# Conditioning products of a small hybrid decoder step: weights held, nine columns streamed, and inputs laid out before the launch

## The chip, the cores and the metric

The kernel runs on one core of a Trainium2 chip. The metric is device time of one execution in microseconds (us), as the median over several runs. The engines are named as the profile names them: PE (TensorE matmul), PEld (its weight loads), DVE (VectorE), ACT (ScalarE), POOL (GpSimd), SP (SyncE, which here only issues DMAs). All data are 32-bit floats.

## The reference

One step of a two-layer decoder on 288 tokens: 256 of a prompt and 32 of eight sequences with four steps each. Layer 0 mixes tokens with a short gated convolution, layer 1 with the RWKV-7 recurrence; behind each stands a product-key expert mixer (PEER). Every sub-layer is scaled, shifted and gated by a vector that depends on the sequence alone:

```
cs = silu(c)                                   # 9 conditioning vectors: 1 prompt, 8 sequences
m = cs @ w_ada[i] + b_ada[i]                   # (9, 1024) @ (1024, 6144), for each of 2 layers
sh_m, sc_m, gt_m, sh_f, sc_f, gt_f = split(m, 6)
h = rmsnorm(x, g_mix[i]) * (1 + sc_m) + sh_m
x = x + gt_m * mixer(h)                        # layer 0: conv, layer 1: RWKV-7
h = rmsnorm(x, g_ffn[i]) * (1 + sc_f) + sh_f
x = x + gt_f * peer_ffn(h)                     # 8 heads x 16 experts a token, rows of 1024 gathered
```

At the end stands one more norm. Outputs are x, the last inputs of the convolution, the last row of layer 1, and the RWKV states (16 heads of 64 x 64, for the prompt and for each sequence).

## The kernel before

Everything is kept with the model dimension on the 128 partitions, in DC = 8 chunks: X and H are [128, 8, 288]. So inputs that arrive as rows of tokens are turned by PE (a product with the identity) and copied out of PSUM, and outputs are turned back.

PE's work is a fixed list of groups (STAGES, line 72). Each group takes the next of four PSUM banks; `done` counts it ready, and ACT or DVE copies it out and frees the bank. Every engine walks the list in the same order. SP loads weight tiles of 1024 x 512 (2 MB) into W, a ring of four (WRING); a tile is loaded when the group that used the slot last is done (line 440).

The conditioning product is split over 24 weight tiles, twelve a layer, in stages ad0 to ad7 (ADA_PARTS, line 62). `ada` on PE (line 501) holds the nine conditioning vectors as weights and streams 512 columns of w_ada, eight chunks deep: L519, eight products a tile, and the trace counts two passes for each 32-bit product. The result has the nine vectors on partitions; ACT copies it to ADR (L967), PE turns it with four small products (L510, `turn`), and ACT adds the bias (L981).

The order is: `crow`, `x`, `par` (turning of inputs, L486 to L498), ad0 (6 tiles), norm 0 (`norm`, L532: eight products with ones), ad1 (8 tiles), the convolution's input projection `cin` (24 groups, `project`, L555), the expert keys turned (`turn_keys`, L540), ad2 (1 tile), output projection `cout`, the convolution's state rows turned (`cst`, L576, copied by ACT at L1040 and sent), norm 1, ad3 (1), the experts of layer 0, norm 2, ad4 (2), the RWKV projections rp, `sst` (last rows turned, L682), kp, vp, the low-rank stages lm and l2 (L691, L700), ad5 (1), kn (L706), ad6 (1), bn (L711), ad7 (4), and the recurrence: two prompt tiles of 128 tokens (stages tm, nm, sq; the final state is turned in `pso`, L860) and the sample tile. There `sq2` works through eight pairs of heads c in an order written out by hand (SQ2, line 87): state blocks arrive in RAW, are turned (L876) and copied by ACT to SS; `right`, `sa`, `y` (L884, L894/L867) and the state update `new0`, `new1` (L901) follow, DVE adds (L1783), and the new states are turned back (L907), copied by ACT to OUTB and sent. Then wo, turn_keys(1), norm 3, the experts of layer 1, norm 4, and `fin`: the result turned (L930), copied (L1243) and sent from ACT (L1247).

The experts gather rows of 4 KB through POOL's queue (L1859); DVE multiplies them (L1451) and PE sums them (L647).

Of the kernel before, what the change touches and what calls it, by code (L numbers as in the profile page):

```python
# [12 lines left out]
P = 128  # L13
# [44 lines left out]
PAR_ROWS = (P, ROWS["b_ada0"] + 48 - P, 48)  # L58
CR_COND, CR_CONV, CR_SHIFT, CR_N = 0, NCOND, NCOND + 2 * NSEQ, NCOND + 3 * NSEQ


ADA_PARTS = {"ad0": [(0, j) for j in range(6)], "ad1": [(0, j) for j in range(6, 10)] + [(1, j) for j in range(4)],
             "ad2": [(0, 10)], "ad3": [(0, 11)], "ad4": [(1, 4), (1, 5)], "ad5": [(1, 6)], "ad6": [(1, 7)],
             "ad7": [(1, j) for j in range(8, 12)]}


def ada_stage(name):
    return [(name, 2 * len(ADA_PARTS[name]))]
# [3 lines left out]
STAGES = [("crow", 1), ("x", DC), ("par", 1), ] + ada_stage("ad0") + [("nrm0", 1)] + ada_stage("ad1")  # L72
STAGES += [("cin", 24), ("kt0", 4)] + ada_stage("ad2") + [("cout", DC), ("cst", 2)]
STAGES += [("nrm1", 1)] + ada_stage("ad3") + [("hf0", 2), ("qa0", 4), ("se0", 1), ("qb0", 12), ("sc0", 9), ("ht0", 4), ("res0", DC)]
STAGES += [("nrm2", 1)] + ada_stage("ad4") + [("rp", DC), ("sst", 2), ("kp", DC), ("vp", DC), ("lm", 3), ("l2", 24)]
STAGES += ada_stage("ad5") + [("kn", DC)] + ada_stage("ad6") + [("bn", DC)] + ada_stage("ad7")
NM_STEPS, NM_STEPS_S = 21, 7
for _t in range(2):
    STAGES += [(f"tm{_t}", 6), (f"nm{_t}a", 2 * NM_STEPS)] + [("gn0", 2)] * (_t == 1)
    STAGES += [(f"nm{_t}b", 2 * NM_STEPS), (f"sq{_t}", 16)] + [("pso", 2)] * (_t == 1)  # L80
STAGES += [("tm2", 6), ("nm2a", 2 * NM_STEPS_S), ("gn1", 2), ("nm2b", 2 * NM_STEPS_S), ("sq2", 9 * DC), ("gn2", 2), ("wo", DC)]
STAGES += [("kt1", 4), ("nrm3", 1), ("hf1", 2), ("qa1", 4), ("se1", 1), ("qb1", 12), ("sc1", 9), ("ht1", 4), ("res1", DC)]
STAGES += [("nrm4", 1), ("fin", 6)]
# [4 lines left out]
for _c in range(-1, DC + 1):  # L88
    SQ2 += [("turn0", _c + 1), ("turn1", _c + 1), ("sa", _c), ("out0", _c - 1), ("out1", _c - 1),
            ("right", _c + 1), ("y", _c), ("new0", _c), ("new1", _c)]  # L90
# [30 lines left out]
def build(nc, a, out):  # L121
    with ExitStack() as ctx:
# [9 lines left out]
        PAR = sb("PAR", [3 * P])  # L132
# [27 lines left out]
        COUT = sb("COUT", [DC, 18])  # L160

# [32 lines left out]
        CROW2 = carve(4 * DC * TOK, [D])  # L194
        YT = carve(2 * DC * TOK, [3, D])
# [13 lines left out]
        ADR = (scr[:].rearrange("p a b -> p (a b)"), DG[:].rearrange("p a b -> p (a b)"))  # L209
# [51 lines left out]
        s_raw0, s_raw = sem("raw_zero"), [sem("raw_loaded0"), sem("raw_loaded1")]  # L261
# [13 lines left out]
        s_silu = sem("silu_ready")  # L275
        s_xready = sem("x_ready")
# [5 lines left out]
        s_crow = sem("conv_rows_ready")  # L282
        s_kt = sem("keys_turned")
# [21 lines left out]
        s_yt = sem("y_rows_ready")  # L305
# [5 lines left out]
        def weight_tiles(w, k, cols, group0, per):  # L311
            for j in range(cols // 512):
                tiles.append(([(None, w[:, j * 512:(j + 1) * 512].rearrange("(c p) m -> p c m", p=P))],
                              group0 + per * (j + 1) - 1))

        def ada_rows(j):

            return max(2 * j - 1, 0)

        def ada_cols(j, n):  # L320
            return 2 * j + 2 if j < n - 1 else 2 * n - 1
# [15 lines left out]
        WT["cin"] = len(tiles)  # L337
        weight_tiles(a["conv_w_in"][0], D, 3 * D, GROUP["cin"], 4)
        ada_tiles("ad2")
        WT["cout"] = len(tiles)  # L340
        weight_tiles(a["conv_w_out"][0], D, D, GROUP["cout"], 4)
        ada_tiles("ad3")
        WT["q0"] = len(tiles)
        weight_tiles(a["peer_wq"][0], D, 2 * D, GROUP["qa0"], 4)
        later_queries(0)
        ada_tiles("ad4")
        for name in ("wr", "wk", "wv"):
            WT[name] = len(tiles)
# [7 lines left out]
        tiles.append(([(lambda _: L2[0:LW_, 0, :], a["rwkv_w2"][0]), (lambda _: L2[0:LA_, 1, :], a["rwkv_a2"][0]),
                       (lambda _: L2[:, 2, :], a["rwkv_g2"][0])], GROUP["l2"] + 23))
        assert WT["wr"] % WRING == 2 and WT["l1"] % WRING == 0 and WT["l2"] % WRING == 1
        for name in ("ad5", "ad6", "ad7"):
            ada_tiles(name)  # L360
        WT["wo"] = len(tiles)
        weight_tiles(a["rwkv_wo"][0], D, D, GROUP["wo"], 4)
        WT["q1"] = len(tiles)
        weight_tiles(a["peer_wq"][1], D, 2 * D, GROUP["qa1"], 4)
# [46 lines left out]
        def _(sp):  # L411
            def rows_in(name, src, n):
                at = ROWS[name]
                sp.dma_start(PR[at % P:at % P + n, at // P, :], src).then_inc(s_par, 16)

# [5 lines left out]
            rows_in("g_mix", a["g_mix"].rearrange("l (c p) -> (l c) p", p=P), 16)  # L421
            rows_in("g_ffn", a["g_ffn"].rearrange("l (c p) -> (l c) p", p=P), 16)
            rows_in("g_final", a["g_final"].rearrange("(c p) -> c p", p=P), 8)
            rows_in("conv_k", a["conv_k"].rearrange("l w (c p) -> (l w c) p", p=P), 24)
            rows_in("rwkv_mix", a["rwkv_mix"].rearrange("l w (c p) -> (l w c) p", p=P), 48)
            for name in ("rwkv_w0", "rwkv_a0", "rwkv_k_k", "rwkv_k_a", "rwkv_lnw", "rwkv_lnb"):
                rows_in(name, a[name].rearrange("l (c p) -> (l c) p", p=P), 8)
            rows_in("rwkv_r_k", a["rwkv_r_k"].rearrange("l (c h) n -> (l c) (h n)", h=2), 8)
            rows_in("b_ada0", a["b_ada"][0].rearrange("(c p) -> c p", p=P), 48)
            rows_in("b_ada1", a["b_ada"][1].rearrange("(c p) -> c p", p=P), 48)  # L430
            def raw(c):

                for hp in range(2):
                    sp.dma_start(RAW[HS * hp:HS * (hp + 1), c % 2, :, HS * hp:HS * (hp + 1)],
                                 a["state_wkv"][0, :, 2 * c + hp].rearrange("b i j -> i b j")).then_inc(s_raw[c % 2], 16)

            for t, (parts, _) in enumerate(tiles):
# [3 lines left out]
                if t == WT["wo"]:  # L441

                    sp.wait_ge(s_raw0, 1)
                    for c in range(2):
                        raw(c)
# [5 lines left out]
                if t == WT["q1"]:  # L451
                    for c in range(2, DC):

                        sp.wait_ge(bank_ready, GROUP["sq2"] + SQ2.index(("turn1", c - 2)) + 1)
                        raw(c)
# [4 lines left out]
            sp.wait_ge(s_out, 16 * 3)  # L460
# [3 lines left out]
        def _(pe):  # L464
# [1470 lines left out]
```

## Time and profile before

| what | value |
|---|---|
| median of 3 runs | 2646.41 us (2644.27 to 2663.16) |
| the profiled execution | 2678.61 us |
| its span, first to last instruction | 2676.9 us |
| mean granted TensorE clock | 0.921 |
| PE busy | 2186.8 us (82%) |
| DVE busy | 1438.0 us (54%) |
| POOL busy | 1197.3 us (45%) |
| ACT busy | 567.2 us (21%) |
| DMA moved | 717 MB, of which the gathers 604 MB |

A busy PE says little by itself: its instructions overlap and their ends are modelled, so the time of a stretch is read from when the next stretch starts. The granted clock is a share of 2.4 GHz: 1.00 is 2.4 GHz, 0.50 is 1.2 GHz, and a figure between them is a stretch with some of each. The chain of waits is followed back from the last instruction, and gives at each step what the next one waited for.

### The profile page before, as it was taken

To read this page: it belongs to the slowest core of one execution; us is meant where nothing else is said; L and a number is where in the kernel's file an instruction comes from. 1 tells how busy PE (TensorE), PEld (TensorE's weight loads), DVE (VectorE), ACT (ScalarE), POOL (GpSimd) and SP (SyncE) were. 2 spreads that over 40 slices of the span, in tenths; PEclk is the share of its full clock that TensorE was granted. 3 is DMA by queue.
4 is the path that set the end of the run, shared out by engine and by line. 5 is a ranking of instruction groups with operands and counts; after the bars stand their busy time and mean duration, and the time that the engine had idled before them with its cause. 6 is when DMAs were issued, how large, how long until landed. Compare 5 with 4: busy or idle time off the path is not lost.

```text
span 2676.9 us, 28048 instructions
## 1 busy us (share of the span) xinstructions
PE 2186.8 (82%) x7875; PEld 1207.3 (45%) x7875; DVE 1438.0 (54%) x3397; ACT 567.2 (21%) x1250; POOL 1197.3 (45%) x1215
## 2 busy tenths in 40 slices
PE   7999976777778777899789998879676767787787
PEld 2276642323323322376279897657332223233234
DVE  0103466677777774322862443745666666777743
ACT  1200222222222221213222211221222222222212
POOL 2000247777777777300000000003577777777772
PEclk9999988989889898999889888989889898898999
DMA  9733569999999999543200000444799999999995
GB/s 320 270 139 133 209 238 386 376 405 410 410 410 410 410 409 405 222 142 131 74 9 1 1 1 5 111 150 147 263 378 378 372 375 388 410 410 410 409 399 195
DMA packets 242643, 717.22 MB, mean 268 GB/s; under 512 B 39673, under 2 KB 45057, under 8 KB 242557
## 3 DMA queue, kind: packets, MB, share of 16 engines
q0 software_dynamic: 165888, 604.05, 58.2%
q1 hardware_dynamic: 62212, 105.00, 11.5%
q10 hardware_dynamic: 14456, 7.06, 1.0%
q8 instruction: 49, 0.80, 0.1%
q14 instruction: 38, 0.30, 0.0%
HBM read 712.38 MB, written 3.65 MB: 267 GB/s over the span
## 4 chain that ended last, share of the span: by engine, by line
PE 59%; DMA 23%; issue 7%; DVE 7%; POOL 2%; ACT 2%; ACTq 0%; DVEq 0%; POOLq 0%; SPq 0%
PE ps L647 24%; PE ps L555 14%; DMA ARENA<-in_peer_v,CURV 11%; DMA ARENA<-in_peer_u,CURU 10%; PE ps L519 6%; PE ps L775 5%; POOL ARENA L1859 2%; PE ps L757 1%; ACT DG L1110 1%; PE ps L617 1%; DVE ARENA L1598 1%; DVE W L1710 1%; PE ps L851 1%; PE ps L825 1%; PE ps L532 1%
## 5 line engine op out<-in xcount | busy, mean ns | idle before, releaser
L647 PE MATMUL ps<-ARENA,DG 128*128 128x512 f32 x2304 | 1140.4, 644 | 386.6 <-ACT DG L1110 259.1
L1859 POOL DMA_INDIRECT ARENA<-in_peer_u,CURU x576 | 584.7, 1015 | 1209.2 <-DVE GX L1421 1017.8
L1451 DVE SCALAR_TENSOR_TENSOR ARENA<-ARENA 128x1024 f32<-128x1024 f32 x576 | 703.5, 1225 | 434.7 <-DMA ARENA<-in_peer_u,CURU 433.2
L647 PEld LDWEIGHTS ps<-ARENA,DG 128*128 128x128 f32 x2304 | 447.8, 204 | 1078.1 <-issue 662.5
L1859 POOL DMA_INDIRECT ARENA<-in_peer_v,CURV x576 | 596.8, 1036 | 228.4 <-issue 139.4
L1110 ACT ACTIVATE DG<-ident,CF 128x128 f32<-128x128 f32 x576 | 219.8, 399 | 825.1 <-PE ps L647 718.9
L555 PE MATMUL ps<-H,W 128*128 128x288 f32 x1024 | 252.1, 409 | 2.8 <-DVEq L1789 2.8
L555 PEld LDWEIGHTS ps<-H,W 128*128 128x128 f32 x1024 | 195.8, 192 | 57.1 <-DVEq L1789 3.0
L519 PE MATMUL ps<-W,CT 128*9 128x512 f32 x384 | 170.4, 598 | 0.0
L775 PE MATMUL ps<-W 128*128 128x128 f32 (+1 forms) x1088 | 127.3, 281 | 0.0
L775 PEld LDWEIGHTS ps<-W 128*128 128x128 f32 (+1 forms) x1088 | 125.1, 196 | 2.3 <-issue 0.9
L555 PE MATMUL ps<-ARENA,W 128*128 128x288 f32 x512 | 124.9, 406 | 0.0
L555 PEld LDWEIGHTS ps<-ARENA,W 128*128 128x128 f32 x512 | 97.0, 190 | 26.6
L967 ACT ACTIVATE W<-ps 128x512 f32<-128x512 f32 (+2 forms) x97 | 55.9, 578 | 231.7 <-PE ps L775 170.7
L967 ACT ACTIVATE ARENA<-ps 128x512 f32<-128x512 f32 (+4 forms) x106 | 54.5, 543 | 197.7 <-PE ps L555 82.7
L1718 DVE TENSOR_TENSOR W<-W,ps 128x512 f32<-128x512 f32 (+1 forms) x76 | 50.6, 666 | 71.5 <-PE ps L775 71.0
L519 PEld LDWEIGHTS ps<-W,CT 128*9 128x9 f32 x384 | 33.5, 91 | 121.9 <-issue 121.6
L757 PE MATMUL ps<-ARENA 64*128 64x128 f32 (+1 forms) x480 | 60.5, 316 | 22.8 <-DVEq L1261 21.1
L1511 DVE TENSOR_TENSOR ARENA<-ARENA,ps 128x1024 f32 (+1 forms) x36 | 44.0, 1221 | 63.1 <-PE ps L647 58.3
L1064 ACT ACTIVATE GX<-GX 128x16 f32<-128x16 f32 x36 | 7.8, 216 | 327.5 <-DVE GX L1421 327.5
L757 PEld LDWEIGHTS ps<-ARENA 64*128 64x128 f32 (+1 forms) x480 | 53.6, 215 | 29.3 <-DVEq L1261 25.9
L1540 DVE SCALAR_TENSOR_TENSOR ARENA<-ARENA,PAR,H 128x288 f32<-128x288 f32 x48 | 21.8, 516 | 81.6 <-PE ps L555 80.6
(281 smaller groups left out, 1646.1 us busy)
## 6 DMA issues: line engine op xcount, KB each, us to landing
W<-in_w_ada SPq DMA_DIRECT2D x24, 2048.0 KB, 8.1
W<-in_peer_wq SPq DMA_DIRECT2D x8, 2048.0 KB, 8.2
W<-in_conv_w_in SPq DMA_DIRECT2D x6, 2048.0 KB, 7.9
ARENA<-in_peer_u,CURU POOLq DMA_INDIRECT x576, 6.6
ARENA<-in_peer_v,CURV POOLq DMA_INDIRECT x576, 6.6
W<-in_conv_w_out SPq DMA_DIRECT2D x2, 2048.0 KB, 7.8
W<-in_rwkv_wr SPq DMA_DIRECT2D x2, 2048.0 KB, 24.9
W<-in_rwkv_wk SPq DMA_DIRECT2D x2, 2048.0 KB, 8.6
```

What stands on the lines that cost most here:

```text
L519: m = pe.matmul(o[0:NCOND, :], CT[:, k, 0:NCOND], W[:, t % WRING, k, :], start=(k == 0), stop=(k == DC - 1))
L532: m = pe.matmul(o[:, 0:TOK], ones[:], SQ[:, c, :], start=(c == 0), stop=(c == DC - 1))
L555: m = pe.matmul(o[:, 0:TOK], W[:, t % WRING, k, (m0 % 4) * P:(m0 % 4 + 1) * P], rhs[:, k, :], start=(k == 0), stop=(k == DC - 1))
L647: m = pe.matmul(ps[:, 4 + 2 * e + i, :], DG[:, k % NDIAG, :], RVV[:, k % RING, i * 512:(i + 1) * 512], start=(k == 0), stop=(k == TOPK - 1))
L757: m = pe.matmul(o[0:n, j * n:(j + 1) * n], head(ops[0], h), head(ops[1], h), start=True, stop=True)
L775: m = pe.matmul(o[0:n, j * n:(j + 1) * n], l[:, j, :], r[:, j, :], start=True, stop=True)
L967: act.activation(dst, src(o), func, **kw).then_inc(free, 1)
L1110: act.activation(DG[:, k % NDIAG, :], ident[:], ACT.Copy, scale=CF[:, e, k:k + 1]).then_inc(s_diag, 1)
L1451: v.scalar_tensor_tensor(RU[:, k % RING, :], RU[:, k % RING, :], 1.0, h, ALU.mult, ALU.mult, accum_out=ZB[:, e, k:k + 1]).then_inc(s_z, 1)
L1511: v.tensor_tensor(oa, oa, ps[:, 4 + 2 * e:6 + 2 * e, :].rearrange("p b n -> p (b n)"), ALU.add).then_inc(acc_free, 1)
L1718: V.do(v.tensor_tensor(dst, dst, o, ALU.add))
L1859: pool.indirect_dma_start(ring[:, k % RING, :], None, tab, bass.IndirectOffsetOnAxis(ap=idx[:, k:k + 1], axis=0)).then_inc(landed[k % RING ...
```

## The change

The conditioning product is turned round: 128 x 128 blocks of w_ada are held as weights and the nine vectors are streamed, four blocks of outputs by eight chunks, that is 32 products of nine columns a tile. The result has the outputs on partitions, so `turn`, ADR and ACT's copy go. The 24 tiles are spread anew: 4 before norm 0, 2 behind it, then after each of the six tiles of `cin` 2, 2, 2, 1, 1, 1, then 1 (ad8), 2 (ad9), 1, 1 and 4 (ad10 to ad12).

kernel() lays out all inputs on the host: weight tiles with 16 KB in one piece for each partition, x, conditioning vectors, keys and parameters already turned, and the sequences' states as blocks of 128 x 1024 with zeros in place. So the stages crow, x, par, kt, cst, sst, pso, turn, out and fin go, with their copies; outputs leave as they lie on the partitions and are turned on the host. In `sq2` five groups are left for each c. SP issues the last output from H in four pieces, each as two chunks of H are ready.

```diff
-ADA_PARTS = {"ad0": [(0, j) for j in range(6)], "ad1": [(0, j) for j in range(6, 10)] + [(1, j) for j in range(4)],
-             "ad2": [(0, 10)], "ad3": [(0, 11)], "ad4": [(1, 4), (1, 5)], "ad5": [(1, 6)], "ad6": [(1, 7)],
-             "ad7": [(1, j) for j in range(8, 12)]}
+ADA_PARTS = {"ad0": [(0, j) for j in range(4)], "ad1": [(0, 4), (0, 5)], "ad2": [(0, 6), (0, 7)], "ad3": [(0, 8), (0, 9)],
+             "ad4": [(0, 10), (0, 11)], "ad5": [(1, 0)], "ad6": [(1, 1)], "ad7": [(1, 2)], "ad8": [(1, 3)],
+             "ad9": [(1, 4), (1, 5)], "ad10": [(1, 6)], "ad11": [(1, 7)], "ad12": [(1, j) for j in range(8, 12)]}
...
+STAGES = ada_stage("ad0") + [("nrm0", 1)] + ada_stage("ad1")
+for _j in range(CIN):
+    STAGES += [(f"cin{_j}", 4)] + ada_stage(f"ad{2 + _j}")
+STAGES += [("cout", DC), ("nrm1", 1)] + ada_stage("ad8")
...
-    SQ2 += [("turn0", _c + 1), ("turn1", _c + 1), ("sa", _c), ("out0", _c - 1), ("out1", _c - 1),
-            ("right", _c + 1), ("y", _c), ("new0", _c), ("new1", _c)]
+    SQ2 += [("sa", _c), ("right", _c + 1), ("y", _c), ("new0", _c), ("new1", _c)]
...
+            sp.dma_start(PAR[:], a["par"]).then_inc(s_par, 16)
+            def states(c):
+                sp.dma_start(SS[:, c % 2].rearrange("p s n -> p (s n)"), a["state_wkv"][c]).then_inc(s_raw[c % 2], 16)
...
-                        sp.wait_ge(bank_ready, GROUP["sq2"] + SQ2.index(("turn1", c - 2)) + 1)
-                        raw(c)
+                        sp.wait_ge(s_kept, c - 1)
+                        states(c)
...
+                if t == WT["q1"] + 1:
+                    for i in range(2):
+                        sp.wait_ge(s_stout[i], 16 * (DC // 2))
...
+            for c in range(0, DC, 2):
+                sp.wait_ge(s_hf, c + 2)
+                sp.dma_start(out["y"][:, c:c + 2, :], H[:, c:c + 2, :]).then_inc(s_out, 16)
...
-                    o = group(stage, ada_rows(j))
-                    for k in range(DC):
-                        m = pe.matmul(o[0:NCOND, :], CT[:, k, 0:NCOND], W[:, t % WRING, k, :], start=(k == 0), stop=(k == DC - 1))
+                    o = group(stage, j)
+                    for m4 in range(4):
+                        for k in range(DC):
+                            m = pe.matmul(o[:, m4 * NCOND:(m4 + 1) * NCOND], W[:, t % WRING, k, m4 * P:(m4 + 1) * P], CT[:, k, 0:NCOND],
+                                          start=(k == 0), stop=(k == DC - 1))
                     done(m)
-                    if j > 0:
-                        turn(j - 1)
-                turn(n - 1)
...
-            project("cin", "cin", 24, H, norm_of=0)
-            turn_keys(0)
-            ada("ad2")
+            for j in range(CIN):
+                project(f"cin{j}", f"cin{j}", 4, H, norm_of=0 if j == 0 else None)
+                ada(f"ad{2 + j}")
...
+            act.dma_start(CT[:], a["cond"]).then_inc(s_cr, 16)
+            act.dma_start(X[:], a["x"]).then_inc(s_x, 16)
...
+                                v.wait_ge(s_raw[c % 2], 16 * (c // 2 + 1))
+                                if c >= 2:
+                                    v.wait_ge(s_stout[c % 2], 16 * (c // 2))
...
+                        v.wait_ge(s_shr, 32)
```

## Rows read from the trace of the kernel before

**Rows 1.** Chain of waits, 0 to 230 us: start us, length us, what.
```profile
3.62 10.47 DMA ARENA<-in_x_sample
...
21.91 14.90 PE ps L519 x32
37.16 6.96 PE ps L519 x16
...
67.19 4.08 PE ps L532 x16
...
130.09 93.32 PE ps L555 x384
```

**Rows 2.** DMA issues of the first 1.25 us: size, us from issue to landing.
```profile
W<-in_w_ada SPq DMA_DIRECT2D x1, 2048.0 KB, 13.1
```

**Rows 3.** Chain of waits, 220 to 420 us.
```profile
233.27 31.24 PE ps L555 x128
264.51 0.45 PE ps L576 x4
...
267.51 4.13 PE ps L532 x16
...
281.46 1.02 PE ps L592 x8
```

**Rows 4.** Chain of waits, 1060 to 1400 us.
```profile
1133.01 13.85 PE ps L519 x32
...
1179.23 0.87 PE ps L682 x8
...
1312.68 14.64 PE ps L519 x32
...
1343.09 2.77 PE ps L733 x24
```

**Rows 5.** Chain of waits, 1441 to 1475 us: 128 x 128 weights, 64 columns streamed.
```profile
1443.33 3.57 PE ps L825 x32
```

**Rows 6.** L775, weight loads ns min/median/max: 1360 to 1365 us, then 1410 to 1415 us.
```profile
L775 PEld LDWEIGHTS ps<-W x20: 286/333/333, 1360.9 to 1364.9; 128*128 128x128 f32 x20
...
L775 PEld LDWEIGHTS ps<-W x46: 186/192/218, 1409.8 to 1415.0; 128*128 128x128 f32 x46
```

**Rows 7.** Windows: stretch, length, busy us (count) PE, PEld, DVE, ACT, POOL, clock, DMA, GB/s.
```profile
20.00:40.00 20.00, 20.00 (x50) 4.93 (x51) 1.48 (x5) 4.55 (x14) 0.35 (x3) 1.00 1.05 373
...
1295.00:1300.00 5.00, 1.91 (x8) 1.14 (x6) 5.00 (x1) 0.56 (x4) 0.00 (x0) 1.00 1.00 356
1300.00:1305.00 5.00, 0.00 (x0) 0.00 (x0) 5.00 (x1) 0.00 (x0) 0.00 (x0) 0.56 0.16 58
1305.00:1310.00 5.00, 1.52 (x3) 1.17 (x4) 4.49 (x6) 0.00 (x0) 0.00 (x0) 0.50 0.00 0
1310.00:1315.00 5.00, 5.00 (x10) 1.78 (x9) 3.68 (x6) 0.00 (x0) 0.00 (x0) 0.57 0.00 0
...
1360.00:1365.00 5.00, 5.00 (x24) 4.78 (x24) 1.47 (x3) 0.89 (x2) 0.00 (x0) 0.50 0.01 3
...
1443.00:1447.00 4.00, 4.00 (x37) 3.99 (x36) 0.00 (x0) 1.25 (x3) 0.00 (x0) 1.00 0.00 0
...
1668.00:1672.00 4.00, 3.73 (x64) 3.40 (x62) 2.73 (x10) 0.00 (x0) 0.00 (x0) 0.50 0.00 0
```

**Rows 8.** Sample tile: chain of waits, then the window 1702 to 1733.5 us.
```profile
1679.05 11.56 DMA ARENA<-in_state_wkv
...
1702.00:1733.50 31.50, 28.93 (x193) 19.42 (x193) 26.13 (x48) 9.26 (x17) 0.00 (x0) 1.00 0.27 59
```

**Rows 9.** Norm 3 in the chain of waits, then the end in the timeline.
```profile
1793.32 4.16 PE ps L532 x16
...
2666.08 3.52 DVE L1310 SCALAR_TENSOR_TENSOR H<-X,PAR,rstd 128x288 f32<-128x288 f32 x8
...
2674.52 0.34 ACTq L1247 DMA_DIRECT2D out<-ARENA  x1
```

More of the change, by code:

```diff
@@ L57 @@
 NROWS = _rows()
-PAR_ROWS = (P, ROWS["b_ada0"] + 48 - P, 48)
-CR_COND, CR_CONV, CR_SHIFT, CR_N = 0, NCOND, NCOND + 2 * NSEQ, NCOND + 3 * NSEQ
-ADA_PARTS = {"ad0": [(0, j) for j in range(6)], "ad1": [(0, j) for j in range(6, 10)] + [(1, j) for j in range(4)],
-             "ad2": [(0, 10)], "ad3": [(0, 11)], "ad4": [(1, 4), (1, 5)], "ad5": [(1, 6)], "ad6": [(1, 7)],
-             "ad7": [(1, j) for j in range(8, 12)]}
-def ada_stage(name):
[L68 to L76, printed above, removed]
+CR_CONV, CR_SHIFT, CR_N = NCOND, NCOND + 2 * NSEQ, NCOND + 3 * NSEQ
+QUAD = 32
+CIN = 6
+ADA_PARTS = {"ad0": [(0, j) for j in range(4)], "ad1": [(0, 4), (0, 5)], "ad2": [(0, 6), (0, 7)], "ad3": [(0, 8), (0, 9)],
+             "ad4": [(0, 10), (0, 11)], "ad5": [(1, 0)], "ad6": [(1, 1)], "ad7": [(1, 2)], "ad8": [(1, 3)],
+             "ad9": [(1, 4), (1, 5)], "ad10": [(1, 6)], "ad11": [(1, 7)], "ad12": [(1, j) for j in range(8, 12)]}
+def ada_stage(name):
+    return [(name, len(ADA_PARTS[name]))]
+STAGES = ada_stage("ad0") + [("nrm0", 1)] + ada_stage("ad1")
+for _j in range(CIN):
+    STAGES += [(f"cin{_j}", 4)] + ada_stage(f"ad{2 + _j}")
+STAGES += [("cout", DC), ("nrm1", 1)] + ada_stage("ad8")
+STAGES += [("hf0", 2), ("qa0", 4), ("se0", 1), ("qb0", 12), ("sc0", 9), ("ht0", 4), ("res0", DC)]
+STAGES += [("nrm2", 1)] + ada_stage("ad9") + [("rp", DC), ("kp", DC), ("vp", DC), ("lm", 3), ("l2", 24)]
+STAGES += ada_stage("ad10") + [("kn", DC)] + ada_stage("ad11") + [("bn", DC)] + ada_stage("ad12")
 NM_STEPS, NM_STEPS_S = 21, 7
@@ L304, in build, with weight_tiles @@
         s_acc = sem("expert_rows_ready")
-        s_yt = sem("y_rows_ready")
         dve_step, pool_step = sem("dve_step"), sem("pool_step")
         tiles = []
[L311 to L321, printed above, removed]
+        def weight_tiles(w, group0, per):
+            for j in range(w.shape[0]):
+                tiles.append(([(None, w[j].rearrange("p (c m) -> p c m", c=DC))], group0 + per * (j + 1) - 1))
         def later_queries(layer):
@@ L355, in build @@
         WT["l2"] = len(tiles)
[L356 to L359, printed above, removed]
+        tiles.append(([(lambda _: L2, a["lora_out"].rearrange("p (c m) -> p c m", c=3))], GROUP["l2"] + 23))
+        assert WT["q0"] % WRING == 0 and WT["wr"] % WRING == 2 and WT["l1"] % WRING == 0 and WT["l2"] % WRING == 1
@@ L360, in build @@
+        for name in ("ad10", "ad11", "ad12"):
             ada_tiles(name)
         WT["wo"] = len(tiles)
-        weight_tiles(a["rwkv_wo"][0], D, D, GROUP["wo"], 4)
+        weight_tiles(a["rwkv_wo"], GROUP["wo"], 4)
         WT["q1"] = len(tiles)
-        weight_tiles(a["peer_wq"][1], D, 2 * D, GROUP["qa1"], 4)
+        weight_tiles(a["peer_wq"][4:8], GROUP["qa1"], 4)
         later_queries(1)
@@ L700, in rwkv @@
                         done(pe.matmul(o[:, 0:TOK], L2[0:n, i, c * P:(c + 1) * P], LM[0:n, i, :], start=True, stop=True))
-                ada("ad5")
+                ada("ad10")
                 pe.wait_ge(s_kksq, 1)
@@ L706, in rwkv @@
                     done(pe.matmul(o[:, 0:TOK], BLK, XI1[:, c, :], start=True, stop=True))
-                ada("ad6")
+                ada("ad11")
                 pe.wait_ge(s_rk, 1)
@@ L853, in rwkv @@
                                 done(m)
-                        if tile == 1:
-                            evac(sq, 12)
-                            evac(sq, 13)
-                            for q in range(2):
-                                o = group("pso", q)
-                                for j in range(4):
-                                    m = pe.transpose(o[:, j * P:(j + 1) * P], SB[:, 4 * q + j, :], ident[:])
-                                done(m)
                     else:
@@ L902, in sample_step @@
                                               SAVM[0:2 * n, 4 * half:4 * half + 4, :].rearrange("p s n -> p (s n)"), start=True, stop=True)
-                            else:
-                                half = int(kind[-1])
-                                evac("sq2", SQ2.index((f"new{half}", c)))
-                                for j in range(4):
-                                    m = pe.transpose(o[:, j * P:(j + 1) * P], NEW[:, c % 2, 4 * half + j, :], ident[:])
                             done(m)
@@ L973, in ada @@
             def ada(stage, between={}):
-                n = len(ADA_PARTS[stage])
-                def columns(j):
-                    o, free = take(stage, ada_cols(j, n))
+                for j, (layer, part) in enumerate(ADA_PARTS[stage]):
+                    o, free = take(stage, j)
                     for m4 in range(4):
-                        layer, m0 = ADA_PARTS[stage][j][0], 4 * ADA_PARTS[stage][j][1]
-                        m = act.activation(ADA[:, layer, m0 + m4, :], o[:, m4 * NCOND:(m4 + 1) * NCOND], ACT.Identity,
-                                           bias=col(f"b_ada{layer}", m0 + m4))
+                        m = act.activation(ADA[:, layer, 4 * part + m4, :], o[:, m4 * NCOND:(m4 + 1) * NCOND], ACT.Identity,
+                                           bias=col(f"b_ada{layer}", 4 * part + m4))
                     m.then_inc(free, 1)
-                for j in range(n):
-                    copy(stage, ada_rows(j), ADR[j % 2][0:NCOND, :], lambda o: o[0:NCOND, :])
-                    if j > 0:
-                        columns(j - 1)
                     if j in between:
                         between[j]()
-                columns(n - 1)
-            taken("par", 0)
+            act.wait_ge(s_par, 16)
             def squares(i):
@@ L1003, in _ @@
             ada("ad0")
-            def keys(layer):
-                for i in range(4):
-                    o, free = take(f"kt{layer}", i)
-                    act.activation(KT[:, i // 2, 4 * (i % 2):4 * (i % 2) + 4, :],
-                                   o.rearrange("p (h k) -> p h k", h=4), ACT.Copy).then_inc(s_kt, 1)
-                    act.wait_ge(s_kt, 4 * layer + i + 1)
-                    act.sem_inc(free, 1)
             def root_and_h(i):
-                if i == 3:
-                    keys(1)
                 act.wait_ge(s_ms, i + 1)
@@ L1026, in _ @@
             ada("ad1")
-            for m in range(16):
-                o, free = take("cin", m)
-                dst = (BG if m < 8 else CG)[:, m % 8, :]
-                act.activation(dst, o[:, 0:TOK], ACT.Copy).then_inc(free, 1)
-                if m == 15:
-                    act.wait_ge(free, (GROUP["cin"] + m) // BANKS + 1)
-                    act.sem_inc(s_gates, 1)
-            keys(0)
-            ada("ad2")
-            for i in range(2):
-                o, free = take("cst", i)
-                if i == 0:
-                    act.wait_ge(s_cv, 1)
-                act.activation(CROW[0:18, i * 512:(i + 1) * 512], o[0:18, :], ACT.Copy).then_inc(free, 1)
-                act.wait_ge(free, (GROUP["cst"] + i) // BANKS + 1)
-            act.dma_start(out[2].rearrange("l b w d -> (l b w) d"), CROW[0:2, :]).then_inc(s_crow, 16)
-            act.dma_start(out[5].rearrange("l b w d -> (l b w) d"), CROW[2:18, :]).then_inc(s_crow, 16)
+            for j in range(CIN):
+                if j < 4:
+                    dst = BG if j < 2 else CG
+                    for m in range(4):
+                        o, free = take(f"cin{j}", m)
+                        act.activation(dst[:, 4 * (j % 2) + m, :], o[:, 0:TOK], ACT.Copy).then_inc(free, 1)
+                    if j == 3:
+                        for m in range(4):
+                            taken("cin3", m)
+                        act.sem_inc(s_gates, 1)
+                ada(f"ad{2 + j}")
+            act.wait_ge(s_cout, 1)
+            act.dma_start(out["conv"], COUT[:]).then_inc(s_crow, 16)
             def experts(layer):
@@ L1048, in experts @@
                 if layer == 0:
[L1049 removed]
+                    ada("ad8")
                 for i in range(2):
@@ L1124, in rwkv @@
                     if stage == "rp":
-                        for i in range(2):
-                            copy("sst", i, CROW2[0:NCOND, i * 512:(i + 1) * 512], lambda o: o[0:NCOND, :])
-                            taken("sst", i)
-                        act.dma_start(out[3][0], CROW2[0:1, :]).then_inc(s_shr, 16)
-                        act.dma_start(out[6][0], CROW2[1:NCOND, :]).then_inc(s_shr, 16)
+                        act.wait_ge(s_sh, 1)
+                        act.dma_start(out["shift"], SHIFT).then_inc(s_shr, 16)
                 copy("lm", 0, LM[0:LW_, 0, :], lambda o: o[0:LW_, 0:TOK], ACT.Tanh)
@@ L1144, in rwkv @@
                 act.activation(XI1, AF, ACT.Square).then_inc(s_kksq, 1)
-                ada("ad5")
+                ada("ad10")
                 act.wait_ge(s_kkn, 1)
                 act.activation(XI0, XI0, ACT.Sqrt).then_inc(s_kkr, 1)
-                ada("ad6")
+                ada("ad11")
                 def exps():
@@ new lines, in rwkv @@
+                            for j in (12, 13):
+                                taken("sq1", j)
+                            act.dma_start(out["wkv_prompt"], SB).then_inc(s_shr, 16)
+                    else:
+                        for c in range(DC):
+                            for k in ("new0", "new1"):
+                                taken("sq2", SQ2.index((k, c)))
+                            act.dma_start(out["wkv_sample"][c], NEW[:, c % 2].rearrange("p s n -> p (s n)")).then_inc(s_stout[c % 2], 16)
@@ L1233, in _ @@
             root_and_h(2)
-            ada("ad4")
+            ada("ad9")
             rwkv()
@@ L1238, in _ @@
             root_and_h(4)
-            for tile in range(3):
-                n = P if tile < 2 else NS_TOK
-                for i in range(2):
-                    o, free = take("fin", 2 * tile + i)
-                    act.activation(YT[0:n, tile, i * 512:(i + 1) * 512], o[0:n, :], ACT.Copy).then_inc(s_yt, 1)
-                    act.wait_ge(s_yt, 2 * tile + i + 1)
-                    act.sem_inc(free, 1)
-                dst = out[0][0, tile * P:(tile + 1) * P, :] if tile < 2 else out[1].rearrange("b t d -> (b t) d")
-                act.dma_start(dst, YT[0:n, tile, :]).then_inc(s_out, 16)
         @block.vector
@@ L1792, in _ @@
             experts(0)
+            gains("ad8", (2,))
             norm(2)
             rwkv()
-            v.wait_ge(s_stout[0], 16 * DC)
-            v.wait_ge(s_stout[1], 16 * DC)
+            for i in range(2):
+                v.wait_ge(s_stout[i], 16 * (DC // 2))
             experts(1)
```

303 lines of the change are left out of this document (94 added, 209 removed).

## The prediction

> **What bounds the kernel now.** I read the chain of waits first, stage by stage, since no engine is the limit throughout. From 22 to 265 us it is PE almost without a break: 14 conditioning tiles, the norm's sum, then `cin` with 93.3 us and, behind one more conditioning tile, `cout` with 31.2 us [rows 1, 3]. A conditioning tile is 16 passes in 6.96 us and a turn of 0.35 us (36.81 to 37.16), so 7.3 us [rows 1]. DMA is not what ends the waits there: at 373 GB/s a 2 MB tile takes 5.6 us [rows 7]. The two gather loops, most of the span, are left alone by the change. Between them lies layer 1 without its experts, where two conditioning tiles (13.85 us) and four (1312.68 to 1343.09, 30.4 us) stand in the chain [rows 4]. The other two, ad5 and ad6, lie beside DVE's work. So 21 of the 24 tiles are on the path, and what one costs decides. The clock view is then the one that matters: it gives PE 1.00 in the dense stretches and 0.50 in others [rows 7].
>
> **The new tile at full clock.** 32 products of two passes are 64 passes, each with a 128 x 128 weight load and nine columns. The nearest row with as many loads is L825, 64 columns: 32 passes in 3.57 us, 0.112 us each, and its loads are no faster where fewer columns stream, so the load is the limit [rows 5]. 64 x 0.112 = 7.15 us, as much as before: the turn goes, nothing else is won.
>
> **The new tile's clock.** Here I see the loss. Before, a pass streamed 512 columns; now it streams nine, for a load that is 14 times as wide, so PE's array sees 576 columns a tile instead of 8192. What such a stretch is granted no row shows. L825's stretch, 64 columns behind each load, keeps 1.00 (1443 to 1447). But from 1668 to 1672 us PE is busy 3.73 of 4.00 us with 64 narrow products (32 columns, 32 or 64 rows) and stays at 0.50 [rows 7]. Being busy is not what raises the clock; streaming much is the nearer reading, and a stream of nine columns is further down than anything that kept 1.00. I take 0.50.
>
> The price there: L775's passes come 24 in 5 us at 0.50, 0.21 us each [rows 7], and its loads take 286 to 333 ns instead of 186 to 192 [rows 6]. I take 0.213 a pass, 13.6 us a tile. Bounds: 0.112 if the load keeps its pace; 0.172 by the shortest loads' ratio (286/186 x 0.112); 0.24 for twice 0.112 and the nine columns behind it.
>
> The Trainium skill ("TensorE: Matmul & The Clock Gate", section LDWEIGHTS) gives a load's time by its columns alone, about columns/1.2 ns, without the clock. For 128 that is 107 ns, near the 112 measured at full clock; it would make a tile 6.8 us at either clock. The longer loads at 0.50 [rows 6] speak against it, though those passes also stream more.
>
> Changes of the clock cost too. PE ends at about 1296.9 us (1.91 busy of the stretch from 1295) and the clock falls at 1300.6 (0.56 over 1300 to 1305): I let 3.7 us, 33 passes, stay fast at the start of a block. PE starts again at 1308.5 (1.52 busy up to 1310), and 1.00 comes back at 1314.3 (0.57 over 1310 to 1315) [rows 7]; I take 5 us at half clock, 2.5 us lost, for each dense stage behind a conditioning block. A block of two tiles is then 3.7 + 95 x 0.213 = 23.9 us, one of one tile 3.7 + 31 x 0.213 = 10.3 us.
>
> **The head.** x, its turning and the rows' turning go, so PE waits for tile 0 alone. It lands 13.1 us after its issue at 0.8 us [rows 2], with the same neighbours in the queues (x, keys): start at 13.9 instead of 21.9 us. Then ad0 4 x 13.6 = 54.4; norm 0 4.1 + 2.3 = 6.4; ad1 23.9; six `cin` tiles 93.3 + 6 x 2.5 = 108.3; blocks 3 x 23.9 + 3 x 10.3 = 102.6. Sum 309.5 us against 233.3 [rows 3]: **+76.2**. The loads, 5.6 us a tile, and ACT's and DVE's work hide behind this. If PE were fast, they still would.
>
> **From cout to rp.** `cout` loses 2.5. `cst` goes: ACT's two copies and two issues held its squares back, so norm 1's sum ended 7.1 us after `cout` (264.5 to 271.6) [rows 3]; without them the last chunk's residual, square and two passes take 2.3: -4.8. ad8 lies beside the norm's work on DVE and ACT, which is all but 1.0 us (copy and turn) of the 9.8 from 271.6 to 281.5 [rows 3]; 2.3 us behind `cout` only its first 12 passes are fast, and 1.4 + 52 x 0.213 = 12.5 us is later than those 9.8 (+2.7). The queries start slow (+2.5): +5.2. ad9: 23.9 instead of 15.0 (1133.0 to 1148), and 2.5 for rp: +11.4. `sst`: -0.9 [rows 4].
>
> **ad10 to ad12.** ad10 and ad11, 10 to 14 us each, still fit beside DVE's work, for which PE waits there today (none of 1300 to 1305 [rows 7]). ad12 follows bn, which runs slow already: 54.4 instead of 30.4, and 2.5 behind it: +26.5. At full clock it would gain 30.4 - 28.6 = 1.8.
>
> **Recurrence, keys, tail.** `pso` and two issues on ACT: -2.5. In `sq2` a round (four in the window, 7.9 us each) loses the turns, but DVE is busy 26.1 of the 31.5 us, 6.5 a round [rows 8]; I take 7.2 with the gaps between its instructions. The stall of 11.6 us for a state behind two weight tiles stays in part, since SP sends the tiles first. Fewer columns a round may also lower the clock. From -9 to +4; I take -4. DVE's new waits (state in, state out, s_shr) have `gated` and `masked` queued behind them; the data are due a round or more earlier. Turning the keys held norm 3's sum back, so that all its 16 passes (4.16 us) stood behind the last square [rows 9] instead of the last two, and ACT's copy before them (0.5): -4.0. At the end H is complete at 2669.6 (DVE 3.52 us from 2666.08), then one issue and a landing of about 2.5 us, 2672.4 instead of 2676.9: -4.5 [rows 9].
>
> **Sum.** 76.2 + 2.5 - 4.8 + 5.2 + 11.4 - 0.9 + 26.5 - 2.5 - 4 - 4 - 4.5 = +101 us. The profiled execution took 2678.6 us; with it 2779.7. It lies 32 us above the median of the runs shown, so the forecast is **2747 us**. At 0.172 a pass the sum is +55 (2701), at 0.24 +132 (2778).
>
> **Rivals.** *The loads count as activity and PE stays at 1.00.* For it: L825's stretch, dense in loads, keeps 1.00 with 64 columns [rows 5, 7]; against: 1668 to 1672. Then the head is 13.9 + 28.6 + 2.5 + 4.1 + 14.3 + 93.3 + 64.4 = 221.1 (-12.2); with -4.8, ad8 -1.0, ad9 -0.7, sst -0.9, ad12 -1.8, pso -2.5, sq2 -8, keys -4, tail -4.5 it is -40: 2606 us, faster. The point from which it decides: whether 64 loads with nine columns behind each hold the clock.
>
> *The clock falls, but a load keeps 0.112 us.* Only the slow starts are lost: head +5.3, cout +2.5, ad8 +1.5, ad9 +1.8, ad12 +0.7, the rest as in the forecast: -9, 2637 us. The row on L775's loads is against it [rows 6]. The rule of the Trainium skill's page cited above would give this one.
>
> *Loads as short as in the turn.* L510 loads nine rows and streams nine columns; four take 0.35 us [rows 1]. If a pass took 0.09, tiles would be 5.6 us, no less than their DMA, and the whole some 30 us under the first rival. Turning and multiplying load differently in L825; little speaks for it.
>
> **Chances.** Forecast 0.62 (its own range 2695 to 2775), clock kept 0.19, load's pace kept 0.14, short loads or something else 0.05. The measurement of this kernel tells about 1% (26 us) from no change. Faster by more than that: 0.22 (the first and the last rival); within: 0.13; slower: 0.65. The range from 2625 to 2775 us leaves out the first and last rivals.
>
> **What would show it.** Right: the windows over ad0 and over the blocks in `cin` show 0.50 and 64 passes in some 13.6 us; `cin` groups start at 0.48 us a pass and go to 0.24; ad12 takes some 54 us; the experts' loops are unchanged. Wrong: 1.00 in ad0, or passes of 0.112 us at 0.50, or PE waiting for weight tiles, which would make the load and not PE the limit.

## The result, and the profile after

The changed kernel takes 2760.09 us (median of 4 runs, 2741.33 to 2776.47) against 2654.78 us for the kernel before measured beside it: a ratio of 1.0408, 95% interval 1.031 to 1.0506. The forecast was 2747 us. Slower, by about the size forecast. The profiled execution is the quickest of the four (span 2739.4 us, mean granted clock 0.876 instead of 0.921).

Chain of waits of the changed kernel (start us, length us, what). L459 is the conditioning product, L487 `project`, L472 the norm's sum; the rows answer to [rows 1, 3, 4, 9].

```profile
0.83 8.26 DMA CT<-in_cond
...
9.63 54.75 PE ps L459 x256
...
70.24 22.77 PE ps L459 x128
93.02 18.53 PE ps L487 x64
111.55 23.09 PE ps L459 x128
...
301.44 33.95 PE ps L487 x128
335.39 3.88 PE ps L472 x16
339.27 8.55 PE ps L459 x64
347.82 1.80 PE ps L518 x8
...
1190.61 23.50 PE ps L459 x128
...
1379.45 51.81 PE ps L459 x256
...
1876.23 3.89 PE ps L472 x16
```

Four tiles of ad0 take 54.75 us, 13.7 a tile. A block of two tiles inside `cin` takes 23.1 us where two tiles took 14.6 before [rows 1], and the dense tile behind a block takes 18.5 instead of 15.6 us (a sixth of the 93.32 us of [rows 1]); from 94 to 98 us, in the first of these, the clock is 0.50.

Windows of the same kernel (stretch, length, busy us with count for PE, PEld, DVE, ACT, POOL, then clock, DMA share, GB/s): ad0, the beginning of ad1 and its middle.

```profile
20.00:50.00 30.00, 30.00 (x143) 30.00 (x142) 0.00 (x0) 1.49 (x8) 0.26 (x3) 1.00 0.63 258
72.00:74.00 2.00, 2.00 (x20) 2.00 (x20) 1.93 (x3) 0.00 (x0) 0.00 (x0) 1.00 0.00 0
86.00:88.00 2.00, 2.00 (x11) 2.00 (x11) 0.00 (x0) 0.00 (x0) 0.00 (x0) 0.50 0.02 8
```

And the weight loads of line 459 (ns min/median/max), in ad0, at the beginning of ad1 and in its middle:

```profile
L459 PEld LDWEIGHTS ps<-CT,W x95: 333/333/334, 29.8 to 49.9; 128*128 128x128 f32 x95
L459 PEld LDWEIGHTS ps<-CT,W x37: 192/192/332, 70.9 to 74.9; 128*128 128x128 f32 x37
L459 PEld LDWEIGHTS ps<-CT,W x39: 333/333/333, 83.8 to 91.9; 128*128 128x128 f32 x39
```

ad1 shows the whole mechanism: right behind the dense norm, at 72 us, the clock is 1.00, a load takes 192 ns and the passes come 0.112 us apart (37 loads from 70.9 to 74.9 us); at 86 us, with PE busy all the while, the clock is 0.50, a load takes 333 ns and the passes come 0.213 us apart (39 loads from 83.8 to 91.9 us). The dense tile behind starts at half clock too. In ad0 the clock column prints 1.00, but loads (333 ns) and passes (54.75 us / 256 = 0.214 us) are those of 0.50. Experiments 1 and 2 below print 1.00 there too, one with fast passes and one with slow ones, so at the start of the span the column is no measurement; the load's length is.

A part of the difference isn't the change's. First and last start of the gather loops' products, before (line 647) and after (line 573):

```profile
L647 PE MATMUL ps<-ARENA,DG x1152: 592/592/1222, 378.5 to 1120.1; 128*128 128x512 f32 x192
L647 PE MATMUL ps<-ARENA,DG x1152: 592/592/1222, 1903.8 to 2650.5; 128*128 128x512 f32 x192
```

```profile
L573 PE MATMUL ps<-ARENA,DG x1152: 592/592/1222, 446.2 to 1178.0; 128*128 128x512 f32 x192
L573 PE MATMUL ps<-ARENA,DG x1152: 592/592/1222, 1987.9 to 2717.7; 128*128 128x512 f32 x192
```

The loops took 741.6 + 746.7 = 1488.3 us in the execution profiled before and 731.8 + 729.9 = 1461.7 after, with the same code. Over the ten profiles of this study they sum to between 1457 and 1512 us, with no relation to the conditioning. So I compare spans without the two loops: 2676.9 - 1488.3 = 1188.6 before, 2739.4 - 1461.7 = 1277.7 after, **+89 us**, where the forecast's sum was +101.

### The profile page after: what moved, and what is told of

Read it like the earlier page. It is cut to its first block, busy times and chain, and to the rows that moved or that the text cites. A ratio compares the mean times of both kernels' runs of the same rounds, so it can differ in the third digit from the quotient of the medians.

```text
span 2739.4 us, 29426 instructions
## 1 busy us (share of the span) xinstructions
PE 2285.5 (83%) x8688; PEld 1450.2 (53%) x8688; DVE 1432.4 (52%) x3385; ACT 526.4 (19%) x1173; POOL 1165.5 (43%) x1215
## 4 chain that ended last, share of the span: by engine, by line
PE 66%; DMA 19%; DVE 7%; issue 5%; POOL 1%; ACT 1%; DVEq 0%; POOLq 0%; ACTq 0%; SPq 0%
PE ps L573 28%; PE ps L487 14%; DMA ARENA<-in_peer_v,CURV 10%; PE ps L459 10%; DMA ARENA<-in_peer_u,CURU 9%; PE ps L693 5%; POOL ARENA L1672 1%; PE ps L675 1%; ACT DG L965 1%; PE ps L472 1%; PE ps L543 1%; PE ps L787 1%; DVE ARENA L1413 1%; DVE W L1523 1%; PE ps L769 1%
## 5 line engine op out<-in xcount | busy, mean ns | idle before, releaser
L1672 POOL DMA_INDIRECT ARENA<-in_peer_u,CURU x576 | 591.4, 1027 | 1307.2 <-DVE GX L1238 1112.0
L1672 POOL DMA_INDIRECT ARENA<-in_peer_v,CURV x576 | 558.4, 969 | 229.3 <-issue 145.3
L459 PE MATMUL ps<-CT,W 128*128 128x9 f32 x1536 | 288.2, 334 | 9.6 <-ACT CT L840 9.6
L459 PEld LDWEIGHTS ps<-CT,W 128*128 128x128 f32 x1536 | 289.3, 296 | 11.0 <-issue 9.6
L487 PE MATMUL ps<-H,W 128*128 128x288 f32 x1024 | 268.3, 427 | 2.8 <-DVEq L1601 2.8
L487 PEld LDWEIGHTS ps<-H,W 128*128 128x128 f32 x1024 | 205.3, 202 | 61.9 <-DVEq L1601 3.0
L487 PE MATMUL ps<-ARENA,W 128*128 128x288 f32 x512 | 129.6, 418 | 0.0
L487 PEld LDWEIGHTS ps<-ARENA,W 128*128 128x128 f32 x512 | 100.4, 197 | 28.4
L845 ACT ACTIVATE W<-ps 128x512 f32<-128x512 f32 (+2 forms) x81 | 46.5, 574 | 192.8 <-PE ps L693 172.0
L675 PE MATMUL ps<-ARENA 64*128 64x128 f32 (+1 forms) x480 | 59.4, 310 | 24.0 <-DVEq L1084 22.6
L845 ACT ACTIVATE ARENA<-ps 128x512 f32<-128x512 f32 (+3 forms) x86 | 43.7, 526 | 182.8 <-PE ps L487 85.2
L856 ACT ACTIVATE ADA<-ps,PAR 128x9 f32<-128x9 f32 x96 | 17.8, 269 | 268.1 <-PE ps L459 268.1
```

The costliest lines, as they stand in the source:

```text
L459: m = pe.matmul(o[:, m4 * NCOND:(m4 + 1) * NCOND], W[:, t % WRING, k, m4 * P:(m4 + 1) * P], CT[:, k, 0:NCOND], start=(k == 0), stop=(k == ...
L487: m = pe.matmul(o[:, 0:TOK], W[:, t % WRING, k, (m0 % 4) * P:(m0 % 4 + 1) * P], rhs[:, k, :], start=(k == 0), stop=(k == DC - 1))
L675: m = pe.matmul(o[0:n, j * n:(j + 1) * n], head(ops[0], h), head(ops[1], h), start=True, stop=True)
L845: act.activation(dst, src(o), func, **kw).then_inc(free, 1)
L1672: pool.indirect_dma_start(ring[:, k % RING, :], None, tab, bass.IndirectOffsetOnAxis(ap=idx[:, k:k + 1], axis=0)).then_inc(landed[k % RING ...
```

## The experiments

All are edits of the changed kernel. `cout` starts at 301.4 us there; that mark shows the head without the loops' scatter.

**1. Streaming more than is needed.** The nine vectors repeated 14 times as the moving operand; the copies are computed and not read.

```diff
+REP = 14
...
-m = pe.matmul(o[:, m4 * NCOND:(m4 + 1) * NCOND], W[:, t % WRING, k, m4 * P:(m4 + 1) * P], CT[:, k, 0:NCOND],
+m = pe.matmul(o[:, m4 * REP * NCOND:(m4 + 1) * REP * NCOND].rearrange("p (r n) -> p r n", r=REP),
+              W[:, t % WRING, k, m4 * P:(m4 + 1) * P], CT[:, k, 0:NCOND].unsqueeze(1).broadcast_to([P, REP, NCOND]),
               start=(k == 0), stop=(k == DC - 1))
...
```

> The changed kernel with the nine vectors streamed 14 times over behind each weight block (126 columns a pass instead of 9); nothing else differs. My theory: the narrow stream let the clock fall and the load takes 0.213 us a pass only because of the clock, so with 126 columns the granted clock is 1.00 in the conditioning blocks, a pass takes 0.112 us, a tile 7.2 us instead of 13.7, cout starts near 217 us instead of 301, ad12 takes 29 us instead of 52, and the whole is about 127 us below the changed kernel (some 2633 us), level with the kernel before or faster. Rival: 128-column loads back to back cost 0.213 us whatever streams behind them: cout at 301 us or later, no gain.

Measured: 2615.58 us (median of 4, 2609.30 to 2656.12), ratio to the kernel before 0.982 (95% interval 0.9728 to 0.9913; so for the ratios below). Chain of waits:

```profile
1.73 18.21 DMA W<-in_w_ada
19.99 21.70 PE ps L460 x192
41.69 3.88 PE ps L474 x16
45.57 14.29 PE ps L460 x128
59.86 15.53 PE ps L489 x64
...
217.30 31.04 PE ps L489 x128
...
1280.69 28.58 PE ps L460 x256
```

Windows of ad0, in its first 4 us and the next 4:

```profile
10.00:14.00 4.00, 4.00 (x21) 4.00 (x20) 0.00 (x0) 1.71 (x6) 3.20 (x13) 1.00 1.02 431
14.00:18.00 4.00, 4.00 (x38) 4.00 (x38) 0.00 (x0) 1.06 (x4) 3.13 (x14) 1.00 1.06 451
```

`cout` starts at 217.3 us, a tile takes 7.14, ad12 28.6. Fourteen times the stream made each pass half as long, 0.112 us, which is also what a pass of nine columns takes while the clock is up (ad1 of the changed kernel): in these runs the load alone sets the pass, and the stream decides at which clock the load runs. The rival (such loads cost 0.213 us whatever follows) falls. The dense tile behind a block is back at 15.5 us. Outside the loops the kernel is 37 us below the one before: what the forecast's first rival gave for a clock that stays up (-40).

**2. Half as many copies**: the same edit with 7 for 14.

> The same with seven copies, 63 columns a pass. My theory: like 126 columns, since the 64-column stretch of the recurrence kept 1.00: cout near 217 us, tile 7.2 us, some 2633 us. Rival: the clock falls gradually with the columns, so the blocks show a figure between 0.50 and 1.00 and cout starts between 230 and 290 us.

Measured: 2641.36 us, ratio 0.9963 (0.9922 to 1.0003). Chain of waits, then a window in ad0, one in ad1, and the loads of the same two stretches:

```profile
9.72 54.84 PE ps L460 x256
...
70.15 14.24 PE ps L460 x128
...
241.82 31.10 PE ps L489 x128
```

```profile
20.00:50.00 30.00, 30.00 (x142) 30.00 (x143) 0.00 (x0) 1.49 (x8) 0.25 (x3) 1.00 0.64 260
70.00:84.00 14.00, 14.00 (x128) 14.00 (x126) 6.67 (x15) 5.20 (x13) 0.00 (x0) 1.00 0.49 187
```

```profile
L460 PEld LDWEIGHTS ps<-CT,W x96: 333/333/334, 29.7 to 50.0; 128*128 128x128 f32 x96
L460 PEld LDWEIGHTS ps<-CT,W x109: 192/192/193, 71.9 to 83.9; 128*128 128x128 f32 x109
```

A miss, and an instructive one. Every block from ad1 on is as fast as with 126 columns (7.1 us a tile), but ad0 is exactly as slow as with nine (54.84 us). Behind a dense stage 63 columns keep the clock up; from a cold start they do not raise it in 55 us. The rival's 230 to 290 us holds the mark, not by its mechanism: no block settles at a clock in between.

**3. The old product in the new order and layout.** Nine vectors held, 512 columns streamed, ACT's copy and `turn` put back; order, layout, `sq2` and outputs as changed.

```diff
+m = pe.matmul(o[0:NCOND, :], CT[:, k, 0:NCOND], W[:, t % WRING, k, :], start=(k == 0), stop=(k == DC - 1))
...
+copy(stage, ada_rows(j), ADR[j % 2][0:NCOND, :], lambda o: o[0:NCOND, :])
```

> The changed kernel with the conditioning product of before (nine vectors held, 512 columns streamed, ACT's copy and the turn), in the new order and with the new layout of inputs and outputs. It tells the turned product from the layout. My theory: the loss is all in the turned product: clock 1.00 in the head, a tile 7.3 us and about 1 us more for each block (the copy and the turn), cout near 226 us, ad12 30 us, some 118 us below the changed kernel (2642 us), that is 10 to 30 us faster than before. Rival: the new order and layout cost time themselves (later loads, blocks inside cin): cout at 240 us or later and the whole slower than before.

Measured: 2631.37 us, ratio 0.9894 (0.9819 to 0.997).

```profile
138.68 13.85 PE ps L477 x32
152.55 0.60 ACT DG L865
153.66 15.72 PE ps L507 x64
...
225.16 31.24 PE ps L507 x128
```

`cout` at 225.2 us, and 24 us below the kernel before outside the loops. So the layout and the order together gain, and the turned product alone loses 113 us on top (1277.7 against 1164.2 outside the loops). The row of ACT between tile and dense group is what the turn costs at the end of a block: 1.1 us pass between the tile's end (152.53) and the dense group (153.66), for copy and turn.

**4. Narrow passes woven into dense ones.** In each `cin` tile the last three groups and the first conditioning tile behind it alternate, product by product.

```diff
+for i in range(3 * DC):
+    m0, k = 1 + i // DC, i % DC
+    m = pe.matmul(oc[m0 - 1][:, 0:TOK], W[:, tc % WRING, k, m0 * P:(m0 + 1) * P], H[:, k, :],
+                  start=(k == 0), stop=(k == DC - 1))
...
+    upto = (i + 1) * 32 // (3 * DC)
+    for m4, ka in mine[taken:upto]:
+        m = pe.matmul(oa[:, m4 * NCOND:(m4 + 1) * NCOND], W[:, ta % WRING, ka, m4 * P:(m4 + 1) * P],
+                      CT[:, ka, 0:NCOND], start=(ka == 0), stop=(ka == DC - 1))
```

> The changed kernel with nine columns, but in the six cin tiles the first conditioning tile behind each is woven into the last three groups of that cin tile: four narrow passes after each three of 288 columns or so. My theory: the clock follows what a whole stretch streams, not the single pass, so it stays at 1.00 there and a narrow pass takes 0.112 us: from the start of cin to cout 175 us instead of 208, some 33 us below the changed kernel. Rival: a load with nine columns behind it takes 0.213 us wherever it stands: no gain in cin.

Measured: 2724.84 us, ratio to the kernel before 1.0253 (1.0176 to 1.0329). A woven stretch (48 dense passes, 64 of nine columns), its window and its loads, then in the chain the second conditioning tile, left alone, and the group behind it:

```profile
99.70:118.60 18.90, 18.87 (x113) 16.39 (x114) 0.00 (x0) 1.07 (x3) 0.00 (x0) 1.00 0.01 3
```

```profile
L515 PEld LDWEIGHTS ps<-CT,W x64: 190/190/193, 100.0 to 118.4; 128*128 128x128 f32 x64
```

```profile
118.65 11.33 PE ps L459 x64
129.98 6.41 PE ps L487 x16
```

Nine columns cost what any load costs when their neighbours are dense: 48 x 0.243 + 64 x 0.112 = 18.8 us, and 18.9 were measured, at 1.00. The rival falls. (0.243 us is a dense pass: 3.88 us / 16.) From the start of `cin` to `cout` it is 187.7 us instead of 208.4, a gain of 21 and not 33: the three tiles left alone still lost the clock (10.8 to 11.3 us each), and the group behind each took 6.4 to 7.0 us instead of 3.9. Outside the loops the whole gains the same 21 us.

**5 to 7. How narrow, once the clock is up.** The edit of number 1 with REP0 = 14 copies in ad0 and REP = 1, 3 or 5 in all later tiles, that is 9, 27 or 45 columns (one run each).

```diff
+r = REP0 if stage == "ad0" else REP
```

> 126 columns a pass in ad0 alone, nine in all later conditioning tiles. It separates the slow start (the clock was never raised in ad0) from the later falls. Theory: ad0 ends near 41.7 us instead of 64.4, and from there all is as in the changed kernel (blocks of two tiles 23 to 24 us, of one 10 to 11 us, each at 0.50 after its first 4 to 6 us): cout at about 279 us. Rival: once raised early, the clock stays up and the later tiles take 7.2 us: cout near 217 us.

> 126 columns in ad0, 27 in all later conditioning tiles. Open which way: if what streams behind a load counts by degrees, 27 columns lie nearer to nine than to 63, and the blocks fall to 0.50 as with nine, cout near 279 us; if any wider stream holds the clock, tiles take 7.2 us and cout starts near 217 us. I take the first.

> 126 columns in ad0, 45 in all later conditioning tiles. 63 columns held the clock once it was up and did not raise it from the start. If 45 hold it too, cout starts near 217 us; if not, the blocks show 0.50 and cout is near 270 to 279 us. I take the first.

Chain of waits of the three (ad1, then `cout`, whose row the view cuts off at 310 us for 9 and 27 columns), and for 45 columns a window inside ad1 as well:

```profile
45.57 24.40 PE ps L461 x128
...
278.40 31.76 PE ps L490 x119
```

```profile
45.63 23.17 PE ps L461 x128
...
277.21 32.82 PE ps L490 x125
```

```profile
45.70 23.79 PE ps L461 x128
...
271.59 32.65 PE ps L490 x128
```

```profile
52.00:68.00 16.00, 16.00 (x77) 16.00 (x77) 1.24 (x6) 3.36 (x10) 0.00 (x0) 0.50 0.37 132
```

9 and 27 came as expected, 45 did not: at 45 columns the clock falls as with nine (27 columns show 0.50 in the same window). The levels have no slope, there are only two: the window of 45 is at 0.50, that of 63 in number 2 at 1.00. When the clock falls does vary a little: with 45 columns two of the later blocks of two tiles took 21.2 and 21.6 us, which is most of why `cout` starts at 271.6 and not at 278.4 us. Starting fast (number 5) moves the head by 23 us and holds nothing later. Its total, 2769.01 us, stands above the changed kernel's median although its head is 23 us shorter: its loops took 742.2 + 769.6 us, 50 more. A single total says nothing here; the marks do.

**8. Wide stream, later keys.** Number 1, with the keys of layer 0 (1 MB) loaded behind norm 0.

```diff
-            load_keys(0)
...
             root_and_h(0)
+            load_keys(0)
             ada("ad1")
```

> 126 columns in all conditioning tiles, and the 1 MB of keys for layer 0 issued behind norm 0 instead of at the start. With 126 columns PE waits in ad0 for the second weight tile until 19.9 us. 1 MB at 430 GB/s is 2.4 us: if the keys stand before that tile, it lands 1 to 2 us sooner and cout starts near 215.5 us instead of 217.3; if the queues serve it regardless, no change. The whole: 2615 us, 1.5% below the kernel before either way.

Measured: 2612.15 us (median of 6), ratio to the kernel before 0.9818 (0.9781 to 0.9855).

```profile
9.54 30.93 PE ps L460 x256
...
216.09 31.04 PE ps L489 x128
```

The wait for the second tile has gone from the chain and `cout` starts at 216.1 us, 1.2 earlier. This is the lowest median measured, 1.8% below the kernel before (interval 1.5 to 2.2%) and 5% below the changed one; by its total alone it can't be told from number 1, only the mark shows the 1.2 us.

## Why the prediction was right

| step | forecast | measured |
|---|---|---|
| a pass, a tile at 0.50 | 0.213, 13.6 us | 0.214, 13.7 us |
| head, to the start of `cout` | +76.2 | +68.2 |
| `cout` | +2.5 | +2.7 |
| norm 1 and ad8, to the turning of H | -2.1 | -4.5 |
| slow starts of the queries, rp and the stage behind ad12; `sst` gone | +6.6 | +5.5 |
| ad9 | +8.9 | +8.5 |
| ad12 | +24.0 | +21.4 |
| `pso` | -2.5 | -2.4 |
| `sq2` and what leads up to it | -4 | -4.0 |
| norm 3 | -4.0 | -2.3 |
| tail | -4.5 | -4.7 |

The deciding step, that nine columns behind each load lose the clock and that the load then takes 0.213 us, is shown: number 1 changes nothing but the columns and gets all of it back. The choice of 0.213 over 0.112 and 0.172 was settled by the traces as well: at 0.50 a load takes 333 ns and a pass 0.214 us with nine columns and with 63 alike, at 1.00 192 ns and 0.112 us. The Trainium skill ("TensorE: Matmul & The Clock Gate", section LDWEIGHTS (loading the stationary operand)) gives a load's time by its columns alone; the traces here do not agree, since the same load of 128 columns took 192 ns at 1.00 and 333 ns at 0.50.

That the total came out so close is in part luck: the medians lie 105 us apart and the forecast's sum was +101, but outside the loops the difference is +89. The forecast's sum was 12 us too high, and the scatter between executions, of which the traces show the loops' part, made up for it.

Three terms were mis-sized, and one of the signs to look for was wrong.

*The start.* I took tile 0's landing time of [rows 2] (13.9 us). Without the turning of x and the rows, what PE waits for is the conditioning vectors, which land at 9.1 (tile 0 is there by then): 4.3 us of the 8 that the head is shorter than forecast. The rest is that a dense group recovers a little sooner (six `cin` tiles 106.5 us for 108.3) and that a block stays fast a little longer: in ad1 the clock falls at about 74.9 us, 4.7 us into the block instead of 3.7 (the last of the 37 loads from 70.9 to 74.9 us takes 332 ns). That also shortens ad12, and ad8 (8.55 us), which was to cost 2.7 us, ends about when H is ready.

*The norms.* That "without them the last chunk's residual, square and two passes take 2.3" was wrong, and so was -4.0 for norm 3. PE takes its work in order, so all 16 passes of the sum stand behind the last dense group, 16 x 0.243 = 3.88 us (335.39 and 1876.23 in the chain above), however early the squares are there. What went is only PE's wait for ACT: 7.1 to 3.9 and 6.2 to 3.9. So norm 1 gave -3.2 and not -4.8; the table's -4.5 is reached only with the 1.3 us that ad8 and the work beside it gave.

*sq2.* The sum held, its parts did not. I took 7.2 us a round without the turns. Two rounds in the chain of the changed kernel, at DVE's masking of SA:

```profile
1802.50 1.23 DVE ARENA L1577
...
1810.39 1.23 DVE ARENA L1577
```

They are 7.89 us apart, as before: in this round DVE's instructions with their gaps fill the time by themselves, and PE's turns were cover, not path. The gain comes from the start, where [rows 8] shows the stall: from the first product of `sq2` to the start of the last update of a state it is 63.6 us now, eight rounds, where it was 68.9. Of these 5.3 us, 1.3 are lost again in the sample tile's steps ahead of `sq2`: from PE's first product there (L757 before, L675 now) to the first of `sq2` it is 25.3 us instead of 24.1.

The term also said that fewer columns a round may lower the clock. They came with a lower one: the sixteen products of `right`, before and after, and a window of the changed kernel over three rounds, where [rows 8] have 1.00:

```profile
1718.80 1.89 PE ps L884 x16
```

```profile
1816.45 3.65 PE ps L787 x16
1802.50:1826.30 23.80, 21.50 (x94) 14.33 (x92) 18.88 (x35) 0.00 (x0) 0.00 (x0) 0.64 0.30 110
```

DVE covers most of this; in the rounds from 1793.79 and from 1818.28 us it waits 1.0 and 1.3 us for PE's updates, and they take 8.7 and 8.0 us. The clock is below 1.00 there in number 1 (0.57 from 1660 to 1675 us) and in number 3 (0.72 from 1670 to 1700 us) as well, so the columns of the conditioning have no part in it; that the missing turns are the cause was not tried by itself.

*What the test would show.* That the windows over ad0 show 0.50 failed as a reading: the column prints 1.00 there, and only the loads' length tells the clock.

Of the difference between the forecast's +101 us and the profiled spans' +62, 27 us are the gather loops, which were that much longer in the execution profiled before.

## What to carry to other kernels

A product that turns a wide stream into many weight loads with a few columns behind each paid twice here: it was bound by the loads (0.112 us a pass at full clock, so no gain over the wide stream), and it lost half of the clock, for itself and for the first microseconds of the dense stage behind it. Where the loads bound the pass anyway, streaming the same columns again (126 in all, here) cost nothing and kept the clock; weaving such passes between dense ones did the same for the passes that were woven. Judge such a change by marks in the chain of waits ahead of the stages that scatter, and by the loads' length where the clock column can't be trusted.

## What had not been expected

Keeping the clock and raising it are different matters. PE was busy without a gap from 9.7 us, and with 63 columns a pass it stayed slow through all of ad0, 55 us, until the dense norm; with 126 columns the passes went from 0.213 to 0.112 us at 14 us. Once up, 63 columns held 1.00 in every later block, and 45 fell to 0.50. That the clock's release follows activity is what the Trainium skill says (the same page, section "Part 1: The HAM clock gate (the "warmup" mystery)"); these runs show that a PE that is always busy is not enough: with 63 columns it was busy for 30.00 of 30.00 us in ad0, and its loads took 333 ns throughout. Why 63 columns hold and do not raise was not tried further.
